# TensorE multiplies constants in five of the pauses that a norm leaves it

## The chip, the cores and the metric

The kernel runs on one core of one Trainium2 chip. The metric is device time in microseconds (us) from the first to the last instruction of one execution, with what the launch adds around it. Before the change it is 1367.97 us, the median of three runs (1366.93 to 1373.21). The core has five engines with queues of their own: TensorE (PE, matrix products and transposes), VectorE (DVE), ScalarE (ACT), GpSimd (POOL, unused here) and SyncE (SP, which issues the weight transfers). TensorE's clock is granted at one of two levels, 1.2 or 2.4 GHz; the profile writes it as a share, 0.50 or 1.00.

## The reference

A sequence of 256 positions with 1024 features goes through one block of a first model and two layers of a second. What matters here is where a whole row must be known before the next product can start:

```
x = x + g1 * (mix @ w_out)
h = rmsnorm(x, norm_mlp_w) * (1 + sc2) + sh2                 # stage "mlp"
x = x + g2 * (square(relu(h @ mlp_w1)) @ mlp_w2)
x = rmsnorm(x, final_norm_w)                                 # stage "fin"
for i in range(2):
    x = layer_norm(ALPHA * x + mixer_i(x), ln1_g, ln1_b)     # "ln1_0", "ln1_1"
    x = layer_norm(ALPHA * x + swiglu(x), ln2_g, ln2_b)      # "ln2_0", "ln2_1"
    x = x + sigmoid(x @ w_gate + b_gate) * (p[i] @ w_proj)   # "ple" after layer 0
```

All data are float32. The output is x after the second layer.

## The kernel before

The residual x lies in SBUF as 128 positions on the partitions, two halves, 1024 features (`x_res`). A product needs the features on the partitions, so in front of every group of products the normed rows `xn` are transposed by TensorE into four PSUM banks, four 128x128 transposes to a bank, 16 in all (`to_feature_form`, line 602; for the stage "ple" it is x itself). ScalarE reads each bank out, with the norm's gain and shift in the same instruction (lines 1011 and 1013), into an SBUF buffer that the trace shows as `arena`. VectorE splits each quarter in two parts, `hT_hi` (line 1395) and `hT_lo` (line 1396), because a float32 product is made of three rounded products: high by high, low by high, high by low (`product3`, lines 538, 543 and 544). The weights come through a ring of five SBUF buffers (`raw`) and are split in the same way, by ScalarE (`w_hi`, line 1028) and VectorE (`w_lo`, line 1378).

Before every transpose stage TensorE has to wait for the norm, which VectorE and ScalarE make from the last products. The semaphore `xn_ready` counts it: VectorE raises it with the last instruction that writes the rows (lines 1425, 1830 or 2002), and the first transpose waits for it. There are eight such stages: "mix" at the start, "mlp", "fin", then "ln1_0", "ln2_0", "ple", "ln1_1" and "ln2_1". In "ln2_0" and "ln2_1" TensorE has other products to make while the norm is computed (the products with `p`, key "pp"), and VectorE splits one tile of weights between the norm and its first `hT` split.

The order on each engine is the order of the code. PSUM's eight banks are handed out in the order of a list, `PLAN`: `begin` takes the next entry and waits on the semaphore `bank_read` of its bank until the entry that had the bank before has been read out. The bank of the first transposes of "ple" is bank 5, and the entry before it in that bank is ("pp", 0, 0): it is read by the first of four multiplications at line 2000, in the very stretch in which TensorE waits for "ple". In "mlp", "fin", "ln1_0" and "ln1_1" the bank was last used by units of attention or by products of the hidden layer, read long before.

`ident` is the 128x128 identity, the first 128 columns of a buffer of constants `const` (`const_sb` in the trace), whose next columns are the masks of the attentions (0 or -1e30).

Of the kernel before, what the change touches and what calls it, by code (L numbers as in the profile page):

```python
# [280 lines left out]
def bank(*key):  # L281
    return PLAN_BANKS[USE[key]]

def read(*key):

    return PLAN_BANKS[:USE[key] + 1].count(bank(*key))

def build(nc, x_in, wstream, pcol_in, prow_in, const_in, p_in, out):  # L290
    ctx = ExitStack()
    with ctx:
        def sb(name, shape):
            return ctx.enter_context(nc.sbuf_tensor(name, shape, F32))

        def sem(name):
            return ctx.enter_context(nc.semaphore(name))
# [23 lines left out]
        const = sb("const_sb", [P, N_CONST])  # L321
# [21 lines left out]
        ident = const[:, CONST["ident"]:CONST["ident"] + P]  # L343
# [121 lines left out]
        xn_ready = sem("xn_ready")  # L465
# [47 lines left out]
        def _(pe):  # L513
            mm = nc.tensor.matmul
            at = [0]

            def begin(*key):

                assert PLAN[at[0]] == key, (PLAN[at[0]], key)
                at[0] += 1  # L520
                if read(*key) > 1:
                    pe.wait_ge(bank_read[bank(*key)], read(*key) - 1)
                return psum[bank(*key)]
# [24 lines left out]
            def chunks(n):  # L548

                splits[0] += n // 2  # L550
# [21 lines left out]
            def token_half(name, n, at_=0, key=None, kn=None):  # L572

                wh, wl, first = tile(name) if kn is None else kn
                vh, vl = (w.rearrange("p (k n) -> p k n", k=DC) for w in (wh, wl))
                b = begin(*key)
                for t in range(TT):
                    for k in range(DC):
                        x_ready(k)
                        last = product3(b[:, t * n:(t + 1) * n], x_part(k, t * P, (t + 1) * P),  # L580
                                        (vh[:, k, at_:at_ + n], vl[:, k, at_:at_ + n]),
                                        k == 0, k == DC - 1, first)
                last.then_inc(psum_full, 1)
# [6 lines left out]
            def gemm_token(name):  # L590

                for j in range(2):
                    token_half(f"{name}.{j}", T, key=(name, j))

            def to_feature_form(stage, n):

                pe.wait_ge(xn_ready, n)
                for j in range(4):
                    b = begin("tr", stage, j)
                    for c in range(2):  # L600
                        for t in range(TT):
                            last = nc.tensor.transpose(
                                b[:, c * T + t * P:c * T + (t + 1) * P],
                                (x if stage == "ple" else xn)[:, t, (2 * j + c) * P:(2 * j + c + 1) * P], ident)
                    last.then_inc(psum_full, 1)
                chunks(DC)
# [101 lines left out]
            pe.wait_ge(ident_loaded, 16)  # L708
            pe.wait_ge(const_loaded, 16)
            to_feature_form("mix", 1)  # L710
            gemm_feature("hf")
            gemm_feature("hq")
# [11 lines left out]
            for c in range(2):  # L724
                b = begin("conv", c)
                for j in range(31):
                    last = mm(b[:, 0:T], tap_matrix(c, j), hpad[:, c * 286 + j:c * 286 + j + T],  # L727
                              start=j == 0, stop=j == 30)
# [14 lines left out]
            for t in range(TT):  # L743
                K = (t + 1) * P
                for j in range(4):
                    b = begin("sc", t, j)
# [12 lines left out]
            b = begin("hgo", 0)  # L759
            for h in range(4):  # L760
                last = mm(b[:, h * P:(h + 1) * P], A_hg[:, h * T:h * T + P], v_hg[:, h * P:(h + 1) * P],
                          start=True, stop=True)
            last.then_inc(psum_full, 1)
            b = begin("hgo", 1)
            for h in range(4):
                mm(b[:, h * P:(h + 1) * P], A1_hg[:, h * P:(h + 1) * P], v_hg[:, h * P:(h + 1) * P],
                   start=True, stop=False)
# [6 lines left out]
            b = begin("cmean")  # L774
# [4 lines left out]
            b = begin("cvar")  # L779
# [3 lines left out]
            for t in range(TT):  # L783
                pe.wait_ge(o_normed, t + 1)
                b = begin("hgt", t)
# [12 lines left out]
            gemm_token("wo1")  # L798

            to_feature_form("mlp", 2)  # L800
            for i in range(8):
                gemm_feature(f"m1_{i}")
# [18 lines left out]

            down(("m2",), [f"m2_{i}" for i in range(16)], hid_hi, hid_lo, 0)
            to_feature_form("fin", 3)

            xn_count = 3
            for layer in range(2):
                if layer == 0:
# [6 lines left out]
                    for j in range(2):  # L834
                        if j == 0:
                            pe.wait_ge(c_normed, 1)
                        b = begin("ct", j)
# [20 lines left out]
                    for t in range(TT):  # L858
                        for n in range(2):
                            b = begin("uq", t, n)  # L860
# [10 lines left out]
                    for j in range(4):  # L871
                        b = begin("uk", j)
# [7 lines left out]
                    for n in range(2):  # L880
                        b = begin("uv", n)
# [7 lines left out]
                    b = begin("krt")  # L889
# [5 lines left out]
                    for j in range(4):  # L895
                        b = begin("qt", j)
# [19 lines left out]
                else:  # L916
# [5 lines left out]
                    b = begin("fd")  # L922
# [30 lines left out]
                for n_ in range(4):  # L953
                    b = begin("pp", layer, n_)
# [396 lines left out]
        def _(dve):  # L1351
# [219 lines left out]
            def decay_factors(lv):  # L1571

                bsz = 1 << (lv - 1)
                dve.wait_ge(decay_exp_done, lv)
                kl, _ = halves(k_hg, bsz)
                _, qr = halves(q_hg, bsz)
                el, er = halves(E_hg[lv % 2], bsz)
                ol, orr = halves(QK[lv % 2], bsz)
                if lv >= 3:
                    dve.wait_ge(psum_full, full("lev", lv - 2, 1))  # L1580
                V.tensor_tensor(ol, kl, el, ALU.mult)
                V.tensor_tensor(orr, qr, er, ALU.mult).then_inc(qk_ready, 1)
                own(qk_ready)
# [560 lines left out]
```

## Time and profile before

| | before |
|---|---|
| median of three runs | 1367.97 us |
| lowest and highest | 1366.93 and 1373.21 us |
| the profiled execution, its own time | 1367.27 us |
| its span, first to last instruction | 1365.5 us |
| TensorE busy | 1181.3 us, 87% |
| VectorE busy | 766.5 us, 56% |
| ScalarE busy | 531.5 us, 39% |
| mean granted TensorE clock | 0.913 |

The times of the profile are counted from the start of the span, and 1.8 us of the execution's own time lie outside it. An engine's busy time is the sum of its instructions. TensorE's instructions overlap (a product's result drains while the next one streams), so a start-to-start distance says more of its pace than the length of an instruction. In the timeline a number in brackets is the idle time of the engine ahead of the row, and the arrow names what ended it.

### The profile page before, as it was taken

To read this page: it belongs to the slowest core of one execution; us is meant where nothing else is said; L and a number is where in the kernel's file an instruction comes from. 1 tells how busy PE (TensorE), PEld (TensorE's weight loads), DVE (VectorE), ACT (ScalarE), POOL (GpSimd) and SP (SyncE) were. 2 spreads that over 40 slices of the span, in tenths; PEclk is the share of its full clock that TensorE was granted. 3 is DMA by queue.
4 is the path that set the end of the run, shared out by engine and by line. 5 is a ranking of instruction groups with operands and counts; after the bars stand their busy time and mean duration, and the time that the engine had idled before them with its cause. 6 is when DMAs were issued, how large, how long until landed. Compare 5 with 4: busy or idle time off the path is not lost.

```text
span 1365.5 us, 19127 instructions
## 1 busy us (share of the span) xinstructions
PE 1181.3 (87%) x8196; PEld 1068.7 (78%) x8196; DVE 766.5 (56%) x969; ACT 531.5 (39%) x705; POOL 0.2 (0%) x4
## 2 busy tenths in 40 slices
PE   4889873749799997994779999998899889999996
PEld 2789872438799886983579999887888579999886
DVE  3562448355677545446557666566544467666556
ACT  4441311042444333337524333343444534333342
POOL 0000000000000000000000000000000000000000
PEclk7799987668999998997789999998999899999998
DMA  9540223712355553640034555542632034444540
GB/s 387 199 140 32 93 93 154 287 83 93 124 185 185 185 190 107 227 148 19 1 124 155 185 185 183 188 156 103 244 130 96 0 124 154 180 181 178 204 155 31
DMA packets 28275, 200.97 MB, mean 147 GB/s; under 512 B 3104, under 2 KB 3616, under 8 KB 5024
## 3 DMA queue, kind: packets, MB, share of 16 engines
q1 hardware_dynamic: 26624, 190.30, 37.9%
q10 hardware_dynamic: 1568, 9.46, 1.8%
q8 instruction: 65, 1.06, 0.3%
q14 instruction: 18, 0.15, 0.0%
HBM read 198.70 MB, written 1.05 MB: 146 GB/s over the span
## 4 chain that ended last, share of the span: by engine, by line
PE 70%; DVE 18%; ACT 6%; issue 3%; DMA 3%; ACTq 0%; DVEq 0%
PE bank L538 20%; PE bank L543 20%; PE bank L544 20%; DVE w_lo L1378 3%; DMA raw<-wstream 3%; PE bank L690 2%; DVE hT_lo L1396 2%; PE bank L727 2%; DVE hT_hi L1395 1%; PE bank L683 1%; PE bank L936 1%; PE bank L935 1%; PE bank L618 1%; ACT w_hi L1028 1%; ACT arena L1048 1%
## 5 line engine op out<-in xcount | busy, mean ns | idle before, releaser
L1378 DVE TENSOR_TENSOR w_lo<-raw,w_hi 128x2048 fp32r<-128x2048 f32 (+1 forms) x159 | 358.0, 2256 | 178.2 <-ACT w_hi L1028 168.5
L1028 ACT ACTIVATE w_hi<-raw 128x2048 fp32r<-128x2048 f32 (+1 forms) x159 | 299.5, 1886 | 332.5 <-PE bank L538 281.1
L538 PE MATMUL bank<-hT_hi,w_hi 128*128 128x256 f32 (+1 forms) x1360 | 393.1, 289 | 16.1 <-DVE w_lo L1378 11.6
L543 PE MATMUL bank<-hT_lo,w_hi 128*128 128x256 f32 (+1 forms) x1360 | 389.9, 287 | 0.0
L544 PE MATMUL bank<-hT_hi,w_lo 128*128 128x256 f32 (+1 forms) x1360 | 389.5, 286 | 0.0
L538 PEld LDWEIGHTS bank<-hT_hi,w_hi 128*128 128x128 f32 (+1 forms) x1360 | 264.9, 195 | 21.1 <-DVE w_lo L1378 13.0
L543 PEld LDWEIGHTS bank<-hT_lo,w_hi 128*128 128x128 f32 (+1 forms) x1360 | 264.9, 195 | 0.2
L544 PEld LDWEIGHTS bank<-hT_hi,w_lo 128*128 128x128 f32 (+1 forms) x1360 | 264.6, 195 | 0.3
L538 PE MATMUL bank<-w_hi,hT_hi 128*128 128x256 f32 (+2 forms) x544 | 160.9, 296 | 27.8 <-DVE w_lo L1378 11.2
L543 PE MATMUL bank<-w_lo,hT_hi 128*128 128x256 f32 (+2 forms) x544 | 157.8, 290 | 0.0
L544 PE MATMUL bank<-w_hi,hT_lo 128*128 128x256 f32 (+2 forms) x544 | 157.4, 289 | 0.0
L538 PEld LDWEIGHTS bank<-w_hi,hT_hi 128*128 128x128 f32 x544 | 108.8, 200 | 33.8 <-DVE w_lo L1378 12.2
L538 PE MATMUL bank<-w_hi,hid_hi 128*128 128x512 f32 x304 | 118.3, 389 | 0.0
L543 PE MATMUL bank<-w_lo,hid_hi 128*128 128x512 f32 x304 | 118.3, 389 | 0.0
L544 PE MATMUL bank<-w_hi,hid_lo 128*128 128x512 f32 x304 | 118.3, 389 | 0.0
L543 PEld LDWEIGHTS bank<-w_lo,hT_hi 128*128 128x128 f32 x544 | 109.1, 201 | 0.2
L544 PEld LDWEIGHTS bank<-w_hi,hT_lo 128*128 128x128 f32 x544 | 108.8, 200 | 0.2
L544 PEld LDWEIGHTS bank<-w_hi,hid_lo 128*128 128x128 f32 x304 | 57.1, 188 | 11.9
L538 PEld LDWEIGHTS bank<-w_hi,hid_hi 128*128 128x128 f32 x304 | 57.1, 188 | 11.9
L543 PEld LDWEIGHTS bank<-w_lo,hid_hi 128*128 128x128 f32 x304 | 57.1, 188 | 11.6
L683 PE MATMUL bank<-const_sb,arena 128*128 128x128 f32 x108 | 24.9, 356 | 31.3 <-ACT arena L1058 25.3
L618 PE MATMUL bank<-raw,tiny 128*32 128x256 f32 x384 | 36.2, 539 | 16.2 <-DVE tiny L1506 9.4
(258 smaller groups left out, 1103.0 us busy)
## 6 DMA issues: line engine op xcount, KB each, us to landing
raw<-wstream SPq DMA_DIRECT2D x179, 1024.0 KB, 4.8
arena<-prow ACTq DMA_DIRECT2D x2, 2560.0 KB, 11.3
x_res<-x ACTq DMA_DIRECT2D x1, 1024.0 KB, 14.9
rows<-prow ACTq DMA_DIRECT2D x2, 512.0 KB, 23.4
out<-x_res SPq DMA_DIRECT2D x1, 1024.0 KB, 4.0
const_sb<-const ACTq DMA_DIRECT2D x1, 872.0 KB, 19.0
raw<-wstream SPq DMA_DIRECT2D x1, 768.0 KB, 4.4
raw<-wstream SPq DMA_DIRECT2D x1, 544.0 KB, 3.7
```

What stands on the lines that cost most here:

```text
L538: ins = mm(o, a[0], b[0], start=start, stop=False)
L543: mm(o, a[0], b[1], start=False, stop=False)
L544: return mm(o, a[1], b[0], start=False, stop=stop)
L618: last = mm(b[32 * g:32 * g + 32, j * T:(j + 1) * T], csil[:, k:k + 1].to_broadcast([P, 32]), w[:, k, :], start=half == 0, stop=half == 1)
L683: last = nc.tensor.transpose(b[:, m * P:(m + 1) * P], p_[:, m * P:(m + 1) * P], ident)
L690: last = mm(b[par * 64:par * 64 + 64, hh * P:(hh + 1) * P], values(4 * g + par + 2 * hh, m), pT_[:, (hh * nb + m) * P:(hh * nb + m + 1) * ...
L727: last = mm(b[:, 0:T], tap_matrix(c, j), hpad[:, c * 286 + j:c * 286 + j + T], start=j == 0, stop=j == 30)
L935: mm(o, negsel[:, h:h + 1].to_broadcast([P, P]), dT[:, 0:K], start=True, stop=False)
L936: return mm(o, qT_c[r:r + 64, c + t * P:c + (t + 1) * P], kT_c[r:r + 64, c:c + K], start=False, stop=True)
L1028: A(w_hi[n % HI][:, 0:m], raw[:, slot % RAW, 0:m], ACT.Copy).then_inc(weights_rounded, 1)
L1378: V.tensor_tensor(w_lo[slot][:, 0:m], raw[:, slot, 0:m], w_hi[n % HI][:, 0:m].bitcast(F32), ALU.subtract).then_inc(weights_split, 1)
L1396: V.tensor_tensor(hT_lo[:, s], src, hT_hi[:, s].bitcast(F32), ALU.subtract).then_inc(input_split, 1)
```

## The change

`to_feature_form` takes its bank first. In five of the eight stages it then issues products of `ident` with the first 512 columns of `const` into that bank, 7 in "mlp", 8 in "fin", 4 in "ln1_0", 4 in "ln1_1" and 6 in "ple", 29 in all. Each is a complete product (start and stop set), and nobody reads it: the 16 transposes that follow overwrite the bank. The wait for `xn_ready` comes after these products. The stages "mix", "ln2_0" and "ln2_1" get none.

```diff
+            idle_products = {"mlp": 7, "fin": 8, "ln1_0": 4, "ln1_1": 4, "ple": 6}
+
             def to_feature_form(stage, n):
 
-                pe.wait_ge(xn_ready, n)
                 for j in range(4):
                     b = begin("tr", stage, j)
+                    if j == 0:
+                        for _ in range(idle_products.get(stage, 0)):
+                            mm(b[:, :], ident, const[:, 0:512], start=True, stop=True)
+                        pe.wait_ge(xn_ready, n)
                     for c in range(2):
                         for t in range(TT):
                             last = nc.tensor.transpose(
```

The queue of TensorE at the stage "mlp", before. The first two rows are the end of the last product of `w_out`; then come the 16 transposes and the first product of the next layer.

```order
L543 MATMUL bank<-w_lo_51,hT_hi 128x256
L544 MATMUL bank<-w_hi,hT_lo 128x256
L602 MATMUL bank<-const_sb,xn 128x128 [waits bank_read5,xn_ready]
L602 MATMUL bank<-const_sb,xn 128x128 x3
L602 MATMUL bank<-const_sb,xn 128x128 [waits bank_read6]
```

The same place with the change. The lines of the kernel move down by 7 from here on, so line 609 is line 602 of before.

```order
L544 MATMUL bank<-w_hi,hT_lo 128x256
L605 MATMUL bank<-const_sb 128x512 [waits bank_read5]
L605 MATMUL bank<-const_sb 128x512 x6
L609 MATMUL bank<-const_sb,xn 128x128 [waits xn_ready]
L609 MATMUL bank<-const_sb,xn 128x128 x3
L609 MATMUL bank<-const_sb,xn 128x128 [waits bank_read6]
```

One wait for two semaphores has become two waits, with seven products between them. "fin", "ln1_0" and "ln1_1" look the same, with 8, 4 and 4 products. The queue of TensorE at the stage "ple", before, where the transposes read x itself and bank 5 comes from the multiplications at line 2000:

```order
L544 MATMUL bank<-w_hi,hT_lo 128x256
L602 MATMUL bank<-const_sb,x_res 128x128 [waits bank_read5,xn_ready]
L602 MATMUL bank<-const_sb,x_res 128x128 x3
L602 MATMUL bank<-const_sb,x_res 128x128 [waits bank_read6]
L602 MATMUL bank<-const_sb,x_res 128x128 x3
```

And with the change:

```order
L544 MATMUL bank<-w_hi,hT_lo 128x256
L605 MATMUL bank<-const_sb 128x512 [waits bank_read5]
L605 MATMUL bank<-const_sb 128x512 x5
L609 MATMUL bank<-const_sb,x_res 128x128 [waits xn_ready]
L609 MATMUL bank<-const_sb,x_res 128x128 x3
```

Here the six products stand behind the wait for bank 5, which ends inside the pause and not at its start. No other engine's queue changes.

## Rows read from the trace of the kernel before

**Rows 1.** The page: the span, and the chain that ended last, by engine.

```profile
span 1365.5 us, 19127 instructions
...
PE 70%; DVE 18%; ACT 6%; issue 3%; DMA 3%; ACTq 0%; DVEq 0%
```

**Rows 2.** Timeline, TensorE's transposes: start us, us, engine line, count, idle before.

```profile
347.51 3.43 PE L602 MATMUL bank<-const_sb,xn 128*128 128x128 f32 x16 [7.13 <-DVE xn L1425]
...
540.06 3.68 PE L602 MATMUL bank<-const_sb,xn 128*128 128x128 f32 x16 [8.18 <-DVE xn L1425]
...
716.74 3.67 PE L602 MATMUL bank<-const_sb,xn 128*128 128x128 f32 x16 [4.70 <-DVE xn L1830]
...
915.16 1.97 PE L602 MATMUL bank<-const_sb,xn 128*128 128x128 f32 x16 [0.26 <-DVE xn L1830]
...
950.33 3.67 PE L602 MATMUL bank<-const_sb,x_res 128*128 128x128 f32 x16 [6.21 <-DVE x_res L2002]
...
1127.63 3.68 PE L602 MATMUL bank<-const_sb,xn 128*128 128x128 f32 x16 [4.69 <-DVE xn L1830]
```

**Rows 3.** Windows, TensorE: stretch, length, PE busy (count), granted clock, DMA share, GB/s.

```profile
347.60:350.50 2.90, 2.90 (x14) 0.50 0.00 0
540.10:545.10 5.00, 5.00 (x22) 0.50 0.24 61
716.80:722.60 5.80, 5.80 (x27) 0.50 0.09 24
950.40:954.70 4.30, 4.30 (x21) 0.50 0.00 0
1127.70:1132.20 4.50, 4.50 (x21) 0.50 0.00 0
```

**Rows 4.** Timeline of stage "ln1_0", from the transposes' first read to the last split.

```profile
717.89 2.84 ACT L1013 ACTIVATE arena<-bank,pcol_sb 128x256 f32<-128x256 f32 x6 [3.05 <-PE bank L602]
...
719.01 0.43 DVE L1395 CAST hT_hi<-arena 128x512 fp32r<-128x512 f32 x1 [2.33 <-ACT arena L1013]
...
722.57 0.43 DVE L1395 CAST hT_hi<-arena 128x512 fp32r<-128x512 f32 x1
...
723.04 0.69 DVE L1396 TENSOR_TENSOR hT_lo<-arena,hT_hi 128x512 fp32r<-128x512 f32 x1
...
723.78 0.39 PE L538 MATMUL bank<-hT_hi,w_hi 128*128 128x256 f32 x1
```

**Rows 5.** Timeline of stage "ln2_0": ScalarE's first reads of the transposes.

```profile
915.86 3.75 ACT L1013 ACTIVATE arena<-bank,pcol_sb 128x256 f32<-128x256 f32 x8 [2.59 <-PE bank L602]
```

**Rows 6.** Windows, TensorE, columns as in rows 3: after "ln1_0", "ln2_0" and "ln2_1".

```profile
724.40:760.00 35.60, 35.17 (x293) 1.00 0.46 165
920.70:923.90 3.20, 2.98 (x15) 0.50 0.02 5
1329.60:1354.60 25.00, 24.00 (x192) 1.00 0.00 1
```

**Rows 7.** Timeline of stage "fin": ScalarE's first reads, VectorE's work ahead of its splits.

```profile
541.22 1.93 ACT L1013 ACTIVATE arena<-bank,tiny,pcol_sb 128x256 f32<-128x256 f32 x4 [2.93 <-PE bank L602]
...
540.04 2.36 DVE L1778 TENSOR_TENSOR x_res<-xn,rows 128x1024 f32<-128x1024 f32 x2
...
542.44 0.43 DVE L1395 CAST hT_hi<-arena 128x512 fp32r<-128x512 f32 x1
```

**Rows 8.** Timeline of the pause before "ple": first and last of eight VectorE instructions.

```profile
944.88 0.69 DVE L2000 TENSOR_TENSOR xn<-bank,xn 128x512 f32<-128x512 f32 x1
...
949.58 0.69 DVE L2002 TENSOR_TENSOR x_res<-x_res,xn 128x512 f32<-128x512 f32 x1
```

**Rows 9.** Float32 products: line 727 by its source line (duration min/median/max), line 781's timeline.

```profile
L727 PE MATMUL bank<-arena x92: 377/378/381, 124.3 to 144.0; 128*128 128x256 f32 x92
...
284.13 2.08 PE L781 MATMUL bank<-arena,avg 128*128 128x256 f32 x4 [6.56 <-DVE arena L1703]
```

**Rows 10.** Windows, TensorE, columns as in rows 3: the stretch of line 727.

```profile
117.40:144.00 26.60, 26.60 (x126) 1.00 0.00 1
```

## The prediction, made before the change was run

> **What bounds the kernel now.** I read the page's chain first: 70% of it is TensorE, 18% VectorE, 6% ScalarE [rows 1]. So an idle stretch of TensorE is time lost, and so is a slow one, unless another engine sets the pace there. Then the timeline of the transposes. In the five stages that the change touches, TensorE stood idle for 7.13, 8.18, 4.70, 6.21 and 4.69 us before them, each time until VectorE had written the rows [rows 2]. The reader is to see two things there. The 16 transposes after such a pause took 3.43 to 3.68 us, and those of "ln2_0", where TensorE had idled for 0.26 us only, took 1.97 us. And the windows say why: in all five, the granted clock was 0.50 (1.2 GHz) from the first transposes on, for 2.9, 5.0, 5.8, 4.3 and 4.5 us of work [rows 3], after pauses in which TensorE did nothing.
>
> The pauses themselves stay. They are made of VectorE's and ScalarE's work on the norm, which the change does not touch. What can be won is only what the low clock costs behind them. For that I read the timeline of one stage as a chain. In "ln1_0" ScalarE starts to read the first bank 1.15 us after the first transpose (717.89 against 716.74) [rows 2, 4]. 1.12 us later VectorE starts the first split (719.01), and the four splits stand 1.19 us apart on average (719.01 to 722.57, three steps), ending at 723.73 (723.04 and 0.69) [rows 4]. TensorE starts the last quarter at 723.78, at once behind it. So in the very stage where the low clock reached furthest into the products (to 722.6) [rows 3], it had caught up by the last quarter: VectorE's splits set the pace up to there, and the low clock on these products cost nothing. Behind it TensorE is busy for 35.17 of 35.60 us at the full clock [rows 6], so what the chain gains up to the last split reaches the end of the program.
>
> **The change, part by part.**
>
> *The products.* A float32 product shows as two instructions. Line 727 makes 62 of 256 columns in sequence and the trace has 92 and 32 records of them; the 92 start between 124.3 and 144.0, that is 19.7 us for 91 steps, 0.2165 us each [rows 9]. 512 columns are four such steps: 0.866 us a product at the full clock. That gives 6.06 us for 7, 6.93 for 8, 3.46 for 4 and 5.20 for 6. The price of the first and the last may be off by some tenths, since no stream of exactly this shape is in the trace. At the half clock the nearest row is line 781: two products of 256 columns, as much work as one of these, in 2.08 us with the drain of the last [rows 9]; twice 0.866 is 1.73 us. I take the full clock, because the products follow at once on dense work, and in the stretch of line 727, which is float32 throughout and whose left operands are diagonal matrices, the granted clock stayed at 1.00 for 26.6 us [rows 10].
>
> *Cover.* In "mlp", "fin", "ln1_0" and "ln1_1" the products lie inside the pause and end 1.07, 1.25, 1.24 and 1.23 us before the rows are there. They cost nothing; without that cover they would cost their length.
>
> *"ple".* Here they wait for bank 5, which the first multiplication at line 2000 gives back at 944.88 + 0.69 = 945.57 [rows 8]. Six end at 950.77, and the transposes began at 950.33 [rows 2]: 0.44 us late. Queued behind them are the transposes, and for these ScalarE and VectorE wait.
>
> *The transposes at the full clock.* ScalarE's first read came 0.70 us after the first transpose in "ln2_0" (915.86 against 915.16) and 1.15 us after it in "ln1_0" [rows 2, 4, 5]. So the chain gains 0.45 us a stage. The rest of the transposes' 1.7 us is no gain, since VectorE's splits are slower than they are. The next thing late is VectorE: its splits start 0.45 us earlier and keep their pace. "mlp", "ln1_0" and "ln1_1": 3 x 0.45 = 1.35 us. "ple": 0.45 - 0.44, nothing. "fin": nothing, since VectorE is at line 1778 until 542.40 and splits from 542.44 on, while ScalarE read from 541.22 [rows 7].
>
> *The products of the next layer.* Nothing up to the last split, as in "ln1_0". Behind it the clock was already 1.00 before.
>
> Sum: 1.35 us. Bounds: 0 if the clock falls all the same; 5 x 0.45 = 2.25 us if "ple" and "fin" had their cover too; for the low clock as a whole see the second rival. Against the profiled execution: 1367.27 - 1.35 = 1365.92 us. The median of the runs stands 0.70 us above that execution, which gives **1366.6 us**.
>
> **The rivals.**
>
> *The fall comes later, on the products (slower side).* The products end about 1.2 us before the transposes, these take 2 us, and then TensorE waits again. "ln2_0" and "ln2_1" show this order with a high clock at the start: in "ln2_0" the clock was 0.50 from 920.7 to 923.9, in the middle of the next products, and in "ln2_1" it was 1.00 throughout [rows 6]. So the traces show both. In the low stretch 15 products started in 3.20 us (0.213 us each), in the high one 293 in 35.60 (0.1215) [rows 6]; over 3.4 us that is 16 in place of 28, 12 x 0.1215 = 1.5 us, of which the part under VectorE's splits costs nothing. Before, the fall lay in the pause, where it is free. Against it speaks that here no weight split stands between the norm and the first `hT` split, so that TensorE's second wait should be shorter than there. One fall turns the gain of 1.35 us into about nothing, two into a loss. One to three: 1367 to 1371 us. All five: at most 1366.6 + 7.5 = 1374.1.
> The stretch "ln2_1" counts against a general fall: the transposes are part of what TensorE did there, and the clock stayed. The Trainium skill, page "TensorE: Matmul & The Clock Gate", section "Part 4: PE-mode transpose", says that transposes do not count as work for the clock; by that rule TensorE would look idle from the last constant product to the first product of the layer, and all five stages would fall late, the 1374 us just given. The trace speaks against the rule.
>
> *The low clock is paid back in full (faster).* 22.5 us of TensorE's work in the five stages ran at half clock [rows 3]; if TensorE alone set the pace, half of it would come back, 11.25 us, and the time would be 1356.7. Against it stands the chain of "ln1_0" [rows 4]. The same page, section "Terms", takes the cost of a low clock as the throttled time times one minus the clock's share; by that the gain would be these 11.25 us. I hold the chain against it: half of that work was waited for by nobody.
>
 At 1.73 us they would end late by 4.98, 5.66, 2.22, 2.23 and, in "ple", 10.38 - 4.76 = 5.62 us: 20.7 us in all, 1388.7 us. It decides from 1.02 us a product on in "mlp" and "fin". Rows 9 and 10 speak against it.
>
> *No effect.* The clock falls between the products' end and the transposes. Then 1368.0, or 1368.4 with the delay in "ple".
>
> **How the numbers follow.** The forecast as worked out, with no fall on the products, 0.55. One to three late falls 0.25, all five 0.04. Paid back in full 0.05. Products at half clock 0.05. No effect 0.06. A difference under 0.5% (6.8 us) can hardly be told from no change here: the three runs before span 0.46%. Within it lie the forecast, the late falls and no effect: same 0.89 (a little of the late falls goes over it). Faster 0.05, slower 0.06. The range takes in the forecast, with some 3 us below it for runs that differ, up to three late falls: 1363 to 1371, which leaves out 0.14 and a part of the late falls.
>
> **What would show it.** In the profile after: groups of 14, 16, 8, 8 and 12 records of 128x512 at line 605, about 0.43 us apart, at a granted clock of 1.00. Transposes of 2.0 us in all five stages. ScalarE's first read 0.7 us after the first transpose, in place of 1.15. In "ple" the transposes start at the sixth product's end, some 5.2 us after the multiplication that frees bank 5. In "fin" VectorE's first split right behind its multiplication, as before. Late falls would show as windows at 0.50 behind the splits. I am wrong if a product takes over 1.02 us, if transposes still take 3.4 us, or if the time falls by more than 3 us: then the low clock on the products was on the path.

## The result, and the profile after

| | before | after |
|---|---|---|
| median (16 runs each, on the same chips) | 1368.92 us | 1378.82 us |
| lowest and highest | 1365.75 and 1373.33 us | 1367.13 and 1386.27 us |
| the profiled execution | 1367.27 us | 1380.63 us |

The ratio of the mean times is 1.0062, 95% interval 1.0039 to 1.0084 (the medians stand 1.0072 to 1): the change makes the kernel slower. The runs of after don't spread evenly: 1367.13, 1367.83 and 1370.41, then 1374.1, and twelve from 1378.34 to 1386.27 us.

The span of after is 1378.8 us. Its page, busy time by engine, and the granted clock over 40 slices of the span:

```profile
PE 1212.1 (88%) x8254; PEld 1079.4 (78%) x8254; DVE 766.8 (56%) x969; ACT 531.3 (39%) x705; POOL 0.2 (0%) x4
...
PEclk8798997668999999997799999999999599999999
```

VectorE and ScalarE do what they did. TensorE is busy for 31 us more (1212.1 against 1181.3), of which the 29 products explain 25; and one slice of the clock's row is a 5, about 1069 to 1103 us, where before has no figure under 6. It lies in none of the five stages.

In the stages themselves the change did what it says. Timeline of after, TensorE, the products and the transposes of "mlp", "fin", "ln1_0", "ple" and "ln1_1" (they answer to [rows 2]):

```profile
341.55 6.17 PE L605 MATMUL bank<-const_sb 128*128 128x512 f32 x14
348.85 1.97 PE L609 MATMUL bank<-const_sb,xn 128*128 128x128 f32 x16 [1.12 <-DVE xn L1432]
...
532.60 7.03 PE L605 MATMUL bank<-const_sb 128*128 128x512 f32 x16
540.94 1.97 PE L609 MATMUL bank<-const_sb,xn 128*128 128x128 f32 x16 [1.31 <-DVE xn L1432]
...
713.23 3.59 PE L605 MATMUL bank<-const_sb 128*128 128x512 f32 x8
718.08 1.97 PE L609 MATMUL bank<-const_sb,xn 128*128 128x128 f32 x16 [1.26 <-DVE xn L1837]
...
946.32 5.42 PE L605 MATMUL bank<-const_sb 128*128 128x512 f32 x12 [1.51 <-DVE xn L2007]
951.58 1.91 PE L609 MATMUL bank<-const_sb,x_res 128*128 128x128 f32 x16
...
1136.58 3.59 PE L605 MATMUL bank<-const_sb 128*128 128x512 f32 x8
1141.44 1.97 PE L609 MATMUL bank<-const_sb,xn 128*128 128x128 f32 x16 [1.26 <-DVE xn L1837]
```

The 16 transposes take 1.91 to 1.97 us a stage where they took 3.43 to 3.68 [rows 2], and the products end 1.1 to 1.3 us before the rows are there, except in "ple". Behind the transposes of "ln1_0", ScalarE's first read and VectorE's last split in after (compare [rows 4]):

```profile
718.78 3.75 ACT L1020 ACTIVATE arena<-bank,pcol_sb 128x256 f32<-128x256 f32 x8 [2.59 <-PE bank L609]
...
723.92 0.69 DVE L1403 TENSOR_TENSOR hT_lo<-arena,hT_hi 128x512 fp32r<-128x512 f32 x1
```

The first read is 0.70 us behind the first transpose (1.15 before), and the last split ends 6.53 us behind it (6.99 before).

Now the place of the loss. The two kernels issue the same instructions but for the products, so each can be found in both traces, and its start in after less its start in before is what has been lost by then. For some of TensorE's instructions (at the first row, up to which the kernels are the same, the two executions already differ by 1.33 us; at 38.9 us it was 0.24, so most of it comes in the course of the program and not with its launch):

| start in before | place | after less before | since the row above |
|---|---|---|---|
| 338.06 | ahead of "mlp" | +1.33 | |
| 360.06 | behind "mlp" | +0.87 | -0.46 |
| 580.01 | behind "fin" | +1.49 | +0.62 |
| 700.00 | ahead of "ln1_0" | +1.34 | -0.15 |
| 740.04 | behind "ln1_0" | +0.88 | -0.46 |
| 940.12 | behind "ln2_0" | +0.70 | -0.18 |
| 975.10 | behind "ple" | +0.76 | +0.06 |
| 1056.01 | attention of layer 1 | +0.76 | 0.00 |
| 1115.10 | behind the attention | +13.80 | +13.04 |
| 1150.08 | behind "ln1_1" | +13.36 | -0.44 |

Up to 1056 us the change has won 0.57 us. Then 13.04 us go in the attention of layer 1, which the diff doesn't touch: 16 units, in each of which TensorE makes logits (lines 942 and 943 of after), transposes probabilities (L690) and multiplies them with the values (L697), while VectorE and ScalarE make the softmax between. Windows of after, TensorE, with the columns of rows 3: the stretch before, the late fall of "fin" and the long low stretch.

```profile
996.00:1058.30 62.30, 61.63 (x428) 1.00 0.30 110
546.40:549.70 3.30, 3.21 (x16) 0.50 0.92 346
1061.90:1099.20 37.30, 37.30 (x105) 0.50 0.00 0
```

The same window of before, all engines (PE, PEld, DVE, ACT, POOL), and then of after:

```profile
1061.90:1099.20 37.30, 31.36 (x147) 20.41 (x146) 16.08 (x43) 16.57 (x54) 0.00 (x0) 0.86 0.00 0
```

```profile
1061.90:1099.20 37.30, 37.30 (x105) 22.57 (x106) 10.74 (x30) 12.18 (x43) 0.00 (x0) 0.50 0.00 0
```

The reader is to see that in after TensorE never stands idle in these 37.3 us and yet gets through 105 instructions in place of 147 (the last six of these belong to the stage behind the attention), and that VectorE and ScalarE do less work (10.74 and 12.18 us against 16.08 and 16.57). The balance of waits has moved: in before TensorE stands idle for 5.9 us of this window, at half clock it never waits, and the softmax waits for it. The waits of after in this window, engine, line, what it waited for, us in total, times, longest:

```profile
DVE arena L1451 <- PE bank L943: 19.3, 6, 4.2
```

In before (lines 1444 and 936 there) it is 12.1 us in 7 waits. And what TensorE did before the clock fell: timelines of TensorE before unit 6, in after, and before unit 10, in before, where the clock falls at 1074.2 for 6.8 us:

```profile
1059.79 0.63 PE L690 MATMUL bank<-const_sb,arena 128*128 128x128 f32 x4 [1.09 <-ACT arena L1065]
```

```profile
1073.62 0.63 PE L683 MATMUL bank<-const_sb,arena 128*128 128x128 f32 x4 [1.09 <-ACT arena L1058]
```

Both times TensorE had stood idle for 1.09 us, waiting for ScalarE's probabilities. In after the clock was still 1.00 from 1059.8 to 1061.8, behind the wait, and 0.50 from there on; in before it fell 0.6 us behind the wait. Before has the same wait at unit 6 too, at 1059.03, and there the clock stays at 1.00 until 1073.9. Why the wait is followed by a fall in the kernel that comes to it 0.57 us earlier in its course, and not in the other, is what the experiments are about.

### The profile page after: what moved, and what is told of

It is laid out like the page before. It is cut to its first block, busy times and chain, and to the rows that moved or that the text cites. A ratio compares the mean times of both kernels' runs of the same rounds, so it can differ in the third digit from the quotient of the medians.

```text
span 1378.8 us, 19238 instructions
## 1 busy us (share of the span) xinstructions
PE 1212.1 (88%) x8254; PEld 1079.4 (78%) x8254; DVE 766.8 (56%) x969; ACT 531.3 (39%) x705; POOL 0.2 (0%) x4
## 3 DMA queue, kind: packets, MB, share of 16 engines
HBM read 198.70 MB, written 1.05 MB: 145 GB/s over the span
## 4 chain that ended last, share of the span: by engine, by line
PE 71%; DVE 17%; ACT 6%; DMA 3%; issue 3%; DVEq 0%; ACTq 0%
PE bank L538 20%; PE bank L544 19%; PE bank L543 19%; DVE w_lo L1385 4%; DMA raw<-wstream 3%; PE bank L697 3%; PE bank L734 2%; DVE hT_lo L1403 2%; PE bank L943 2%; PE bank L690 1%; PE bank L942 1%; DVE hT_hi L1402 1%; PE bank L625 1%; ACT w_hi L1035 1%; DVE x_res L1848 1%
## 5 line engine op out<-in xcount | busy, mean ns | idle before, releaser
L690 PE MATMUL bank<-const_sb,arena 128*128 128x128 f32 x108 | 25.7, 364 | 30.3 <-ACT arena L1065 24.2
L1055 ACT ACTIVATE arena<-arena,tiny 128x128 f32<-128x128 f32 (+1 forms) x56 | 25.0, 447 | 67.9 <-DVE tiny L1459 67.9
```

The costliest lines, as they stand in the source:

```text
L690: last = nc.tensor.transpose(b[:, m * P:(m + 1) * P], p_[:, m * P:(m + 1) * P], ident)
L1055: last = A(L, L, ACT.Exp, bias=negmax[:, m + hh:m + hh + 1], accum_out=rowsum[:, m + hh:m + hh + 1])
```

## The experiments

Every kernel computes the same outputs: what they add, products of constants or a multiplication on VectorE, is read by nobody. All are timed beside the kernel before. "Attention" below is the change of the attention's length against before's profile, the start of an instruction at 1115.10 us of before less that of one at 1056.01, as in the table above; it belongs to the one profiled execution, the median to all. Theory A: what decides is where the attention of layer 1 comes to lie; small shifts ahead of it move it against the clock's own course, so that a wait of 1.09 us is followed by a fall or not. Its rivals: B, TensorE's additional products themselves bring the clock down later; C, executions differ by chance and the kernels don't. In the first expectations the letters are narrower: A is the lateness of "ple", in e4 the place in time alone, and B is that the other four stages bring the loss. The change itself was timed once, beside its own runs of before, so a difference between it and an experiment is one between two rounds, whose medians of before lie between 1368.27 and 1369.03 us.

C in its plain form falls on the times alone: the 130 executions of before on record end at 1374.49 us, and twelve of the change's sixteen begin at 1378.34.

**The products of "ple" alone, without them, and five.**

```diff
-            idle_products = {"mlp": 7, "fin": 8, "ln1_0": 4, "ln1_1": 4, "ple": 6}
+            idle_products = {"ple": 6}                                             # e1
+            idle_products = {"mlp": 7, "fin": 8, "ln1_0": 4, "ln1_1": 4}           # e2
+            idle_products = {"mlp": 7, "fin": 8, "ln1_0": 4, "ln1_1": 4, "ple": 5} # e3
```

> Products only in the stage ple (6 of them). Theory A (ple's lateness): the transposes of ple start later, the attention of layer 1 moves by some 0.7 us against the steps of the clock, and falls into a long stretch at 1.2 GHz: most executions 10 to 13 us above the kernel before, as with all five stages. Theory B (the four other stages bring it, by moving the program ahead of layer 1 or by TensorE's extra work there): no long low stretch, within 1.5 us of the kernel before. Theory C (chance: the clock's steps lie anywhere against the program, and 12 slow executions of 16 are luck): slow executions in any kernel, the one before too.

> Products in mlp, fin, ln1_0 and ln1_1, none in ple. Theory A: no long low stretch in the attention of layer 1; three stages gain 0.45 us each, 1.3 us faster than the kernel before. Theory B: 9 to 12 us slower, as with all five. Theory C: a mixture here and in the kernel before.

> All five stages, but 5 products in ple in place of 6, so that they end before the rows are there and the transposes start at once, at the full clock: ple 0.4 us shorter than before the change, not 0.7 us longer. Theory A (lateness in ple): no long low stretch, some 1.7 us faster than the kernel before. If the high clock in ple itself is to blame and not the lateness, or by theory B: still 9 to 12 us slower.

Measured, beside 1368.48 us: 1369.73 us alone (ratio 1.0014, 0.9993 to 1.0034; attention +2.98), 1366.66 without them (1.0011, 0.9982 to 1.0040; attention +0.05; eight of twelve runs up to 1368.0, four from 1373.7 to 1384.0), and 1361.85 with five (0.9960, 0.9945 to 0.9975; attention -2.86). A as recorded asked e1 for 10 to 13 us and got 1.3; it held in e2 and e3, where B as recorded missed. With five products in "ple" the change beats the kernel before, by 6.6 us. So a single product taken from "ple" changes the time by 17 us, and the six products alone cost next to nothing. That "ple" comes late by some tenths is not the cause by itself: its local effect is +0.06 us. B, read as these six products, would have them cost about what the change costs, and they don't.

**A delay without any products.** One more VectorE multiplication of 128x512, 0.69 us, in the pause ahead of "ple", in the kernel before:

```diff
+                    if layer == 0 and n == 3:
+                        link(V.tensor_tensor(sb_suffix, sb_suffix, suffix_mask, ALU.mult))
```

> The kernel before, without any product, but with one more VectorE instruction (128x512, multiplied into a buffer nobody reads) in the pause before ple, so that everything behind it is 0.7 us late, with the clock low in the pause as before. Theory A in its plain form (only the place in time counts): most executions 10 to 13 us slower. If it takes TensorE's products: 0.7 us slower and no long low stretch. Theory C: a mixture.

Measured 1374.92 us (1.0051, 1.0033 to 1.0069), 6.4 us for an instruction of 0.7 us; the expectations had 10 to 13 us by A and 0.7 by its rival. In its profile, 5.3 us over that of before, 1.5 us go ahead of the attention's count, between 975 and 1056 us, with a fall of the clock at 1001.9 that before has not, and 3.54 in the attention, with this window:

```profile
1077.10:1090.60 13.50, 13.50 (x39) 8.23 (x39) 3.58 (x10) 4.27 (x15) 0.00 (x0) 0.50 0.00 1
```

A low stretch of 13.7 us where before has 6.8, with no product of constants anywhere: B cannot be the whole cause.

**The same delay added to the change, once and twice.**

```diff
+                    if layer == 0 and n == 3:
+                        for _ in range(1):    # e6: range(2)
+                            link(V.tensor_tensor(sb_suffix, sb_suffix, suffix_mask, ALU.mult))
```

> The changed kernel with one more VectorE instruction (128x512, nobody reads it) in the pause before ple: the rows are there 0.7 us later, the transposes of ple start some 0.3 us later than in the changed kernel. Place theory (what counts is where the attention of layer 1 lies against the steps of the clock, and the 12 us of the changed kernel are one such place): the added delay leads out of the bad place, the long low stretch is gone or rarer, median under 1374 us although work was added. Rival (TensorE's extra products wear the clock down, the place doesn't matter): 1379 us or a little more.

> The same with two such instructions: the transposes of ple start some 1.0 us later than in the changed kernel. Place theory: again another place, no long low stretch of 30 us or more, 1368 to 1376 us. Rival: 1380 us or more, slower than with one.

Measured, beside 1368.27: 1370.16 us with one (1.0010, 0.9994 to 1.0025) and 1373.98 with two (1.0041, 1.0028 to 1.0054); attention +3.25 and +4.55. Adding work to the chain makes the change 8.7 us quicker (8.0 with each beside its own before); more of it gives some back. The clock still falls behind the wait of unit 6, but comes back after 13.7 us (second row: the whole window at 0.50):

```profile
1058.10 0.63 PE L690 MATMUL bank<-const_sb,arena 128*128 128x128 f32 x4 [1.08 <-ACT arena L1065]
```

```profile
1060.00:1073.50 13.50, 13.50 (x40) 8.14 (x38) 3.58 (x10) 4.19 (x15) 0.00 (x0) 0.50 0.00 0
```

**Products of constants in the attention.** Ahead of the transposes of units 6, 10 and 14, where TensorE waits for 1.09, 1.09 and 2.75 us, one, one and three products, in the change (e7), with five in "ple" (e8), in the changed kernel with none in the five stages, which stands for before (e9), and in this with the delay of e4 (e10).

```diff
+                        if name == "fox":
+                            for _ in range({6: 1, 10: 1, 14: 3}.get(i, 0)):
+                                mm(b[:, :], ident, const[:, 0:512], start=True, stop=True)
```

> The changed kernel with five more products of constants, in layer 1's attention, where TensorE waits for the probabilities even at the full clock: one ahead of the transposes of unit 6, one of unit 10, three of unit 14. If the 12 us lie in that attention running at 1.2 GHz: the clock stays at 2.4 GHz there, the stretch from the first to the last unit is 13 us shorter than in the changed kernel's profile, and the median is 1362 to 1366 us. If something else slows it: 1379 us plus up to 4 us for the products.

> As the run before, with 5 products in ple in place of 6. If the clock in the attention is held up by the five products there, the place no longer matters: the same time as the run before less 0.4 to 2 us, with a narrow spread. If the gain of the run with five products in ple was that of its place alone, this kernel is not faster than 1361.9 us by more than 2 us.

> The kernel before with the five products in layer 1's attention (units 6, 10 and 14) and none in the five stages. If the attention's clock is what varies from kernel to kernel: it stays high there, 2.5 to 4.5 us less than the kernel before, about 1364.5 us, with a narrow spread. If the gain with both kinds of products came from the stages: no gain.

> The same with the late rows in ple (one more VectorE instruction, 0.7 us). Without the attention's products this lateness cost 6.6 us in the median. Place theory: what it cost beyond its own 0.7 us was the clock in the attention, so here it costs 0.5 to 2 us against the run with the products alone. Otherwise again 5 us or more.

| | before beside it | this | ratio, 95% | attention |
|---|---|---|---|---|
| e7: change, units filled | 1368.27 | 1363.48 | 0.9960 (0.9947 to 0.9974) | -3.92 |
| e8: the same, five in "ple" | 1368.27 | 1361.28 | 0.9945 (0.9930 to 0.9961) | -4.08 |
| e9: before, units filled | 1368.29 | 1363.71 | 0.9964 (0.9950 to 0.9979) | -4.16 |
| e10: e9 with the delay | 1368.29 | 1364.56 | 0.9981 (0.9964 to 0.9998) | -4.59 |

Window of e7 and of e9:

```profile
1059.00:1096.10 37.10, 34.85 (x174) 21.24 (x175) 18.04 (x49) 20.18 (x65) 0.00 (x0) 1.00 0.01 2
```

```profile
1059.00:1096.00 37.00, 34.90 (x175) 21.36 (x174) 17.44 (x48) 20.07 (x68) 0.00 (x0) 1.00 0.00 0
```

With its clock held up in the attention the change is 15.3 us quicker, and it then stands level with the kernel before treated in the same way (1363.48 and 1363.71): the five groups of the change are worth 0.2 us, within what can be told apart. And the delay that cost 6.4 us costs 0.85 here, about its own length. So the loss of the change, and what the delay costs beyond its own length, come in the main through the clock in the attention. The executions are also closer together (1361.91 to 1364.50 in e7, against 1367.13 to 1386.27), but for one of e10 at 1371.93.

**The best of them, and the change without the products of "fin".**

```diff
+            idle_products = {"mlp": 7, "ln1_0": 4, "ln1_1": 4, "ple": 5}   # e11, with the units filled
+            idle_products = {"mlp": 7, "ln1_0": 4, "ln1_1": 4, "ple": 6}   # e12
```

> Products in mlp (7), ln1_0 (4), ln1_1 (4) and ple (5), none in fin, and the five in the attention: the stages' 3 to 4 x 0.45 us, no late fall behind fin (0.7 us), and a high clock in the attention. 1360 to 1362.5 us, the fastest.

> The changed kernel without the products in fin, nothing in the attention. The fall of the clock goes back into the pause before fin, 0.7 us are saved behind it, and the attention gets another place. By the place theory the time is not bound to be 0.7 us less: anywhere from 1361 to 1381 us, and the profile must show the whole difference to the changed kernel beyond 1 us as low clock in the attention of layer 1. If a kernel with such a profile has its difference elsewhere, the theory falls.

Measured, beside 1368.29: e11 1361.23 us (0.9953, 0.9939 to 0.9967), 7.1 us under the kernel before, of which 4.6 come from the attention's five products alone (e9). It can't be told from e8 (1361.28) and e3 (1361.85). e12 1381.17 us (1.0078, 1.0051 to 1.0105), attention +13.99, with 47.8 us at half clock:

```profile
1061.50:1109.10 47.60, 45.56 (x131) 27.25 (x132) 13.38 (x37) 16.20 (x54) 0.00 (x0) 0.50 0.00 0
```

In "fin" the late fall is gone (against before the kernel goes from +1.18 to +1.03 there, the change from +0.87 to +1.49), and the kernel is not quicker for it. Eight products in "fin" do not always bring that fall either: the profiles of after, e2, e3, e5, e6, e7, e15 and e16 have it, those of e8 and e13 have the clock at 1.00 there.

**Does the clock go down at the wait of unit 6, and do the products of "ple" take part?** The change and e2 come to the attention at the same place, within 0.03 us (0.57 and 0.60 us ahead of before, counted from 338 us on), and yet differ by 12 us. Four more kernels: one product ahead of unit 6 alone (e13), neither "fin" nor "ple" (e14), four products in "ple" (e15), and e2 with the delay (e16).

```diff
+                            for _ in range({6: 1}.get(i, 0)):                             # e13
+            idle_products = {"mlp": 7, "ln1_0": 4, "ln1_1": 4}                            # e14
+            idle_products = {"mlp": 7, "fin": 8, "ln1_0": 4, "ln1_1": 4, "ple": 4}        # e15
+            idle_products = {"mlp": 7, "fin": 8, "ln1_0": 4, "ln1_1": 4}                  # e16, and the VectorE instruction
```

> The change with one product of constants ahead of the transposes of unit 6 of the attention of layer 1, where TensorE stands idle for 1.09 us at 1059.8, just before the 37.5 us at half clock. Theory (the low clock is entered at this wait and then kept, since at half clock the vector engines wait for TensorE): the stretch from 1061.8 is gone, short ones of 3 to 7 us may stay further on; attention 10 to 13 us shorter, median 1366 to 1369. Rival (the low clock there has nothing to do with this wait): median 1377 to 1381.

> The change without the products of ple and without those of fin: mlp 7, ln1_0 4, ln1_1 4. Its attention lies where that of the kernel without fin's products lies (1381.2 with ple's products, 47.8 us at half clock). If the place of the attention alone decides, 1379 to 1382 here too. If the products in ple take part in what happens 110 us later, as the pair of the change and the kernel without ple's products suggests (same place within 0.05 us, 1378.8 against 1366.7), 1365 to 1369.

> The change with 4 products in ple: they end about 1.2 us before the rows are there, so nothing comes late, and the attention moves ahead by the 0.45 us of the transposes. If it is the presence of products in ple that brings the low clock in the attention, 1377 to 1381 as with six; if it is the place, the 1361.9 of five products (transposes on time in both), 1361 to 1364; if it is only that six products leave no gap ahead of the transposes, about 1366.

> The kernel without ple's products (1366.7) with one more VectorE multiplication in the pause ahead of ple, 0.7 us. If the place alone decides, a time other than 1366.7 by several us in one direction or the other, since the attention lies 0.7 us later (near that of the kernel before, 1368.3, or of the kernel before with the same delay, 1374.9). If the low clock from 1061 on needs the products in ple, no stretch longer than 7 us begins at 1061, and the median lies between 1366 and 1371.

| | this (before: 1369.03) | ratio, 95% | attention |
|---|---|---|---|
| e13 | 1365.58 | 0.9971 (0.9956 to 0.9986) | -3.12 |
| e14 | 1378.42 | 1.0043 (1.0010 to 1.0076) | +0.07 |
| e15 | 1363.39 | 0.9962 (0.9948 to 0.9975) | -2.85 |
| e16 | 1369.82 | 1.0007 (0.9993 to 1.0020) | +2.97 |

One product at one wait (e13) takes 13.2 us off the change (forecast 1366 to 1369 us), and all of its twelve runs lie at 1368.47 or below. Window of e13, from before that wait to the next fall:

```profile
1057.00:1087.00 30.00, 26.16 (x131) 15.90 (x130) 14.02 (x41) 17.14 (x60) 0.00 (x0) 1.00 0.00 1
```

e14 has no product in "ple" at all and its median is that of the change. But its twelve runs are 1364.4 to 1366.6 (five) and 1378.1 to 1383.9 (seven), with nothing between, and its profile shows an execution of the first sort, at full clock past unit 6:

```profile
1059.00:1073.80 14.80, 13.71 (x72) 8.70 (x70) 7.05 (x20) 8.35 (x31) 0.00 (x0) 1.00 0.00 0
```

The seven have a mean granted clock of 0.899 to 0.913 and the five of 0.919 to 0.925, so the loss goes with a low clock again, but none of the seven was profiled, and that it lies in the attention is not shown. If it does, the products of "ple" are not needed for it. So the same program goes either way, some 15 us apart, and what the kernels change is how often. Read in this way, the change (three or four of 16 near before), e2 (eight of twelve) and e14 (five of twelve) are one group. My number for e14 by place alone, 1379 to 1382, took one outcome for granted and missed for the same reason. e16 stayed near before, with the low stretches of e1; its 1 us against before is inside the interval.

Over all kernels without products in the attention, by where the attention of the profiled execution lies against before, counted from 338 us on (a minus is earlier):

| place | kernels | attention |
|---|---|---|
| -1.11 and -1.05 | e3, e15 | -2.86, -2.85 |
| -1.29 | e12 | +13.99 |
| -0.61 to -0.57 | e14, e2, after | +0.07, +0.05, +13.04 |
| -0.40 | e5 | +3.25 |
| 0.00 to +0.14 | before, e1, e16 | 0, +2.98, +2.97 |
| +1.82 and +2.19 | e6, e4 | +4.55, +3.54 |

e3 and e15, e14 and e2, e1 and e16 agree to 0.02 us, though their products and delays differ, and figures of both signs stand half a microsecond apart. That is what theory A asks for. (Counted from 338 us on, because only so do they fall together: what happens up to there shifts e3 and e15 by 3.0 us against each other.) Against it stand three places: before beside e1, 0.02 us apart with 0 and +2.98; the row of after; and e12 beside e3.

The traces also allow a count from the clock itself, which takes one of the three away. The last low stretch ahead of the attention begins 87.1 us before the instruction counted here in after, e2, e12 and e14 alike (87.08 to 87.16; in after at 969.6, in e12 at 969.3), and 55.9 us before it in e3 and e15. So e12 belongs with after and not with e3. Before and e1 come to lie 0.13 us apart (87.63 and 87.76). What stays is the one place of 87.1 us, where two profiles lose 13.0 and 14.0 us and two lose under 0.1. Place, as far as a trace shows it, does not settle the outcome alone.

Place also belongs to an execution and not only to a kernel. At 700 us, counted from 338 us on, eight profiles with the change's code up to there (after, e2, e3, e5, e6, e7, e15 and e16) lie within 0.07 us of before, but e13 lies 0.84 us ahead and e8 2.07. So the seven long executions of e14 may have come to another place than its profile.

## Why the prediction was wrong

I forecast 1366.6 us, in the range of 1363 to 1371, and "same" with 0.89. It was 1378.82 and slower.

*The products.* Right: 14, 16, 8, 8 and 12 records, 0.429 us apart, 0.858 us a product against 0.866, at a granted clock of 1.00. The rival of half clock had nothing in it.

*Cover and "ple".* Right: the gaps ahead of the transposes are 1.12, 1.31, 1.26 and 1.26 us (forecast 1.07 to 1.25), and "ple" came out at +0.06 against nothing. That five products there would keep the 0.45 us is seen in e3, where, counted against before, the splits gain 0.45 us on the rows (2.32 us early against 1.87).

*The transposes at full clock.* Right: "mlp", "ln1_0" and "ln1_1" gave 0.46, 0.46 and 0.44 us, 0.45 forecast for each, with ScalarE's first read at 0.70 us. That the low clock is paid back in full, the second rival, was right to be left: these three gave 1.36 us.

*"fin".* Mis-sized: not nothing, but +0.62 us net. VectorE's first split stood right behind its multiplication, as said (543.31, with the multiplications ending at 543.28), and then came a late fall, the window from 546.4 above. It is the first rival, in one stage, at 0.81 us where 1.5 was the price, of which the next stretch, by 570 us, gave back 0.19. The other four stages had none. The rule of the Trainium skill, page "TensorE: Matmul & The Clock Gate", section "Part 4: PE-mode transpose", that transposes don't count as work for the clock, would have it in all five; the trace shows it in one and not in four. Unforeseen was "ln2_0": the fall of before at 920.7 [rows 6] did not come, which gave 0.18 us net.

*The step that failed.* "What the chain gains up to the last split reaches the end of the program." The sum took everything behind a stage to move as one piece, and the clock of later stretches to stay as in the profile before. Up to 1056 us it held: 0.57 us were gained, where the sum had 0.90 by then. The reading behind it was one window of 35.6 us after "ln1_0" [rows 6]. Then the attention, entered 0.57 us earlier in the program's course, ran 37.5 us at half clock and lost 13.04. No rival had a price for a stretch outside the five stages, though before's own low stretches there, at 1074.2 (6.8 us) and 1091.3 (3.4 us), and its runs up to 1373, were to be seen. The bound on all late falls, 1374.1, priced each as one short stretch of 3.4 us; here a single stretch lasted 37.5 us.

*What is shown and what is not.* Shown: the loss of the change lies in the attention and comes through the clock there (its own profile, e7, e13; e9 and e10 for the kernel before and the delay); a delay with no product at all costs 6.4 us, most of it through the clock (e4), and a delay added to the change makes it quicker (e5), so the number of TensorE's products is not the cause. Argued only: that it is the place against the clock's own course that picks the outcome, and, since none of e14's seven long executions was profiled, that the products of "ple" are not needed. Not settled: why the stretch, once begun, lasted 37.5 us; what in one execution makes it go the one way or the other at the same place; and so why the change and e12 take the longer time in most of their executions and e2 in a third.

By the Trainium skill, page "TensorE: Matmul & The Clock Gate", section "Terms", the price of a low clock is the throttled time times one minus the clock's share. Spans and mean clocks of the two profiles give 0.087 x 1365.5 = 118.8 us before and 0.083 x 1378.8 = 114.4 after, that is, 4.4 us less for the change; it took 13.3 us more. The mean clock went up while the kernel got slower, so it was no guide here to what the clock costs.

## What to carry to other kernels

A stretch in which TensorE is busy but waits about 1 us now and then for engines it alternates with is where a small shift far upstream can cost or win ten times its size, as here 0.57 us and 13; look at its granted clock, and look at single runs and not at the median alone, before pricing a change of half a microsecond. Filling just those waits (here five products of constants, 4.3 us of work nobody waits for) was worth 4.6 us; filling the long pauses of 5 to 8 us besides was worth 0.2 us with the change's numbers (e7 against e9) and 2.5 with those of e11, because there VectorE's splits hide most of what the low clock costs. An instruction added or taken off as a pure delay is a cheap test of whether a change acts by what it does or by where it puts the rest.

## What was not expected of the hardware

- The clock, once down in the attention, did not come back for 37.5 us in after and 47.8 us in e12, with TensorE busy for 37.30 of 37.30 and 45.56 of 47.60 us. The same work ran at 1.00 in e7 and e9, from 1059 to 1096 us.
- In after and e5 the long stretch began about 2 us behind a wait of 1.09 us, in work that was otherwise close together; one product of 0.86 us in that wait, and the stretch was gone (e13).
- One program's executions can fall into two groups 15 us apart (e14), two profiles can lie at one place against the clock's last fall and differ by 13 us (after and e2), and the mean clock of a better kernel (0.915 in e9) can lie below that of a worse one (0.917 in after).
